# Delta net chunk inverse: from doubling levels on TensorE to a block series whose 32x32 diagonal blocks VectorE solves column by column

## The reference

```python
xn = rmsnorm(h, attn_norm)
proj = xn @ w_in               # columns: q, k, v, z, a, b, sB, sC, sh, gA, gB
qkv = silu(causal_dwconv(qkv, width 4)); q, k = l2norm(q), l2norm(k)
G = jnp.cumsum(g, axis=-1)     # log decay in a chunk
decay = jnp.exp(jnp.where(lower, G[..., :, None] - G[..., None, :], -jnp.inf))
A = jnp.where(strict, beta[..., :, None] * kk * decay, 0.0)
sol = lax.linalg.triangular_solve(eye + A, rhs, left_side=True, lower=True)
u, w = sol[..., :Dv], sol[..., Dv:]
...                            # per chunk: u_new, output o, state S; then o = rmsnorm(o) * silu(z)
h = h + mixed @ w_o            # then SwiGLU FFN and a per-layer embedding
```

## Time and profile before

| | |
|---|---|
| median of 3 runs | 2937.09 us (2936.52 to 2937.82) |
| profiled execution (its span) | 2936.8 us; the profile gives no other time for this execution |
| period of the loop `groups` | 150.7 us, 7 times |
| busy in the span | PE 97%, PE's weight loads 95%, DVE 59%, ACT 46%, POOL 5% |

### The profile page before, as it was taken

The page is one execution under the profiler, slowest core; times in us unless marked ns, Lnnn a source line. Parts: engine busy times, 40 slices in busy tenths (PEclk is TensorE's granted clock), DMA queues, the critical chain, the costliest instruction groups (busy, mean ns, idle before and its releaser), DMA issues.

```text
span 2936.8 us, 60061 instructions
## 1 busy us (share of the span) xinstructions
PE 2862.6 (97%) x22925; PEld 2803.5 (95%) x22925; DVE 1725.2 (59%) x3042; ACT 1342.0 (46%) x1999; POOL 141.7 (5%) x240
## 2 busy tenths in 40 slices
PE   6999999999999999999999999999999999999997
PEld 5999999999999999999999999999999999999997
DVE  5665565656566565655333555555677666776664
ACT  5434444444444443434334444334556544665563
POOL 2000000000000000000000000000011000100000
PEclk9999999999999999999899999999999999999998
DMA  6534343434333333437665555574799666995551
GB/s 208 169 98 126 107 127 110 125 105 121 111 117 118 111 112 119 123 117 217 182 197 171 175 172 172 172 261 145 223 315 294 209 207 188 317 300 183 174 169 63
DMA packets 435904, 494.13 MB, mean 168 GB/s; under 512 B 17329, under 2 KB 419498, under 8 KB 432866
## 3 DMA queue, kind: packets, MB, share of 16 engines
q1 hardware_dynamic: 415264, 415.42, 45.3%
q0 software_dynamic: 19872, 75.90, 8.2%
q10 hardware_dynamic: 578, 0.19, 0.0%
HBM read 467.67 MB, written 24.36 MB: 168 GB/s over the span
## 4 chain that ended last, share of the span: by engine, by line
PE 93%; DVE 3%; ACT 1%; issue 1%; DMA 0%; DVEq 0%; ACTq 0%
PE bank L579 93%; DVE wlo L1116 1%; ACT xhi L853 0%; DVE cacc L1272 0%; DVE GW L1255 0%; DMA vrow<-in_gdn_norm 0%; PE bank L627 0%; ACT whi L839 0%; DVE h L1534 0%; DVE xlo L1137 0%; ACT pp L993 0%; DVE hpro L1129 0%; DVE o_all L1260 0%; DVE cin L1333 0%; DVE xlo L1144 0%
## 5 line engine op out<-in xcount | busy, mean ns | idle before, releaser
L579 PE MATMUL bank<-xhi,whi 128*128 128x264 f32 x5520 | 1614.7, 293 | 43.2 <-issue 23.0
L579 PE MATMUL bank<-xlo,whi 128*128 128x264 f32 x5520 | 1584.1, 287 | 0.0
L579 PE MATMUL bank<-xhi,wlo 128*128 128x264 f32 x5520 | 1580.7, 286 | 0.0
L1116 DVE TENSOR_TENSOR wlo<-raw,whi 128x1024 fp32r<-128x1024 f32 x828 | 1007.8, 1224 | 799.2 <-ACT whi L839 797.2
L839 ACT ACTIVATE whi<-raw 128x1024 fp32r<-128x1024 f32 x828 | 874.4, 1059 | 788.7 <-PE bank L579 785.0
L579 PEld LDWEIGHTS bank<-xhi,whi 128*128 128x128 f32 x5520 | 1056.8, 191 | 61.0 <-issue 53.7
L579 PEld LDWEIGHTS bank<-xlo,whi 128*128 128x128 f32 x5520 | 1057.2, 192 | 4.5 <-issue 3.8
L579 PEld LDWEIGHTS bank<-xhi,wlo 128*128 128x128 f32 x5520 | 1054.8, 191 | 0.0
L579 PE MATMUL bank<-GW 128*128 128x128 f32 x2432 | 294.1, 275 | 0.0
L579 PEld LDWEIGHTS bank<-GW 128*128 128x128 f32 x2432 | 283.2, 192 | 0.0
L579 PE MATMUL bank<-ahi,wlo 128*128 128x264 f32 x704 | 200.1, 284 | 0.0
(11 more groups left out here) (259 smaller groups left out, 1655.6 us busy)
## 6 DMA issues: line engine op xcount, KB each, us to landing
raw<-in_w_in SPq DMA_DIRECT2D x356, 512.0 KB, 3.7
raw<-in_w_ffn_gate SPq DMA_DIRECT2D x88, 512.0 KB, 4.5
raw<-in_w_ffn_up SPq DMA_DIRECT2D x88, 512.0 KB, 4.8
raw<-in_w_ffn_down SPq DMA_DIRECT2D x96, 384.0 KB, 3.8
raw<-in_w_gdn_out SPq DMA_DIRECT2D x64, 512.0 KB, 3.5
chunkS<-in_state_gdn POOLq DMA_DIRECT2D x16, 1024.0 KB, 7.4
raw<-in_w_sconv_out SPq DMA_DIRECT2D x32, 512.0 KB, 3.6
raw<-in_w_o SPq DMA_DIRECT2D x32, 512.0 KB, 3.6
```

The source lines that it names most:

```text
L579: return pe.matmul(out, lhsT, rhs, start=start, stop=stop)
L1116: dve.tensor_tensor(wlo[:, at_ % SPLIT, :, :], raw[:, at_ % RAW, :, :], f32(whi[:, at_ % SPLIT, :, :]), ALU.subtract).then_inc(lo_ready, 1)
```

## The change

**Inverse.** The strictly lower triangular matrix of a chunk is split in its four 32x32 diagonal blocks and the rest. The diagonal blocks of all 8 systems (4 heads, 2 chunks) are laid over the 128 partitions by a DMA round trip through DRAM on ACT's queue (`blk_store`, `blk_load`). DVE solves them by forward elimination with 31 pivots, each as a multiplication and an addition over two halves of the columns (4 instructions for a pivot, 124 in all), four pivots after each of the pieces 17 to 24. POOL brings the result back through DRAM (`solution_out`) as `DT`, and PE multiplies it with what lies below the diagonal blocks (`pt`); the right hand side is then applied as a short series of four terms in that product (`pt0`, `pe0`, `pf0` for chunk 0, `pt1`, `pe1`, `pf1` for chunk 1).

**Order.** Pairs in the loop come as q, k, v0, v1, z, sC, sh, z. The tables have two parts: `cur` for the head group whose columns this iteration streams (pieces 9 to 31) and `prev` for the one before (pieces 0 to 6). **Tiles.** `GW` gives way to `E`, `Tt`, `QK`, `Nn`, `PT`, `DT`, `blk`, `sol`, `prod`; the weight ring shrinks from 8 to 4 slots.

```diff
-RAW = 8
+RAW = 4
...
+SB = 32
+QC = 8
...
-QKVS = ("v0", "v1", "q", "k")
+def layer_pairs(gx):
+    return [qkvpair(k, gx) for k in ("q", "k", "v0", "v1")] + [zpair(0, gx), spair("sc", SC0, gx), spair("sh", SH0, gx), zpair(1, gx)]
...
-LEVELS = {p: (p - 3,) for p in range(8, 20)}
-PE_STEP = {0: (0,), 1: ("decay",), 2: (1,), 5: (3,), 7: (4,), **LEVELS, 20: (17, 23), 21: (18,), 22: (19,), 23: (20,),
-           24: (21,), 26: (22,)}
...
+PE_STEP = {"cur": {9: ("decay",), 10: ("sums",), 12: ("kkqk",), 14: ("nturn",), 18: ("tails",), 19: ("vturn",), 26: ("pt",),
+                   27: ("pt0",), 28: ("pe0",), 29: ("pf0",), 30: ("s1",), 31: ("ks",)},
+           "prev": {0: ("t1",), 1: ("pt1",), 2: ("pe1",), 3: ("pf1",), 4: ("o1",), 5: ("osum",), 6: ("sct",)}}
+ACT_STEP = {"cur": {10: ("squares",), 11: ("root", "exps"), 13: ("kcopy",), 14: ("blk_store",), 15: ("ncopy",), 16: ("blk_load",),
+                    19: ("stage",), 20: ("vcopy",), 26: ("t0c",), 28: ("f0c",), 30: ("s1c",)},
+            "prev": {0: ("t1c",), 2: ("f1c",), 4: ("osq",), 5: ("oroot",), 7: ("sct",)}}
+DVE_STEP = {"cur": {9: ("gsel",), 10: ("exponents",), 12: ("qkn",), 13: ("lt",), 26: ("mask",), 27: ("e0",), 28: ("ktok",),
+                    29: ("u0",), 31: ("r",)},
+            "prev": {1: ("e1",), 3: ("u1",), 4: ("s2",), 7: ("o",)}}
+PER_PIECE = 4
+for n in range(-(-(SB - 1) // PER_PIECE)):
+    b = 17 + n
+    DVE_STEP["cur"][b] = DVE_STEP["cur"].get(b, ()) + (f"solve{n}",)
...
 # PE
+elif slot == "pt":
+    pe.wait_ge(tails_staged, gr + 1)
+    pe.wait_ge(g["vcopied"], gr + 1)
+    pe.wait_ge(g["dt_in"], gr * 64 + 64)
...
 # ACT
+elif slot == "blk_store":
+    act.wait_ge(g["lt"], gr + 1)
+    for b in range(4):
+        act.dma_start(blk_d[:, b, :, :].rearrange("m j i -> j m i"), ...).then_inc(g["blk_stored"], 16)
+elif slot == "blk_load":
+    act.wait_ge(g["blk_stored"], gr * 64 + 64)
+    for q in range(4):
+        act.dma_start(blk[SB * q:SB * q + SB, :, :]..., ...).then_inc(g["blk_in"], 16)
...
 # DVE
+elif slot.startswith("solve"):
+    if n0 == 0:
+        dve.wait_ge(g["blk_in"], gr * 64 + 64)
+        for hc in halves:
+            chain.inc(dve.tensor_copy(sol[:, hc, :], unit[:, hc, :]))
+    for j in range(n0, min(n0 + PER_PIECE, SB - 1)):
+        n = SB - 1 - j
+        for hc in halves:
+            chain.settle(dve, but=1)
+            chain.inc(dve.tensor_tensor(prod[:, hc, 0:n], blk[:, j, j + 1:SB]..., sol[:, hc, j:j + 1]..., ALU.mult))
+        for hc in halves:
+            chain.settle(dve, but=1)
+            m = chain.inc(dve.tensor_tensor(sol[:, hc, j + 1:SB], sol[:, hc, j + 1:SB], prod[:, hc, 0:n], ALU.add))
...
 # POOL
+def solution_out(grp):
+    pool.wait_ge(g["solved"], grp + 1)
+    for q in range(4):
+        pool.dma_start(sol_d[:, :, QC * q:QC * q + QC, :]..., sol[SB * q:SB * q + SB, :, :]...).then_inc(g["sol_stored"], 16)
+    pool.wait_ge(g["sol_stored"], grp * 64 + 64)
+    for b in range(4):
+        pool.dma_start(DT[SB * b:SB * b + SB, :, SB * b:SB * b + SB], ...).then_inc(g["dt_in"], 16)
```

More of the change, by code:

```diff
@@ L242, in trunk @@
         g = {n: sem("g_" + n) for n in (
-            "squares", "gsel", "sums", "log", "gb", "root", "dt", "qkn", "kkqk", "turned", "copied",
-            "lt", "lt_turned", "vturned", "x", "y", "ycopied", "xy", "u0", "u0s", "s1", "s1c", "ks", "r",
-            "expo", "xinit", "u1", "u1s", "o1", "s2", "stored", "osq", "osum", "olog", "oroot", "o")}
+            "squares", "gsel", "sums", "log", "gb", "root", "expo", "dt", "qkn", "kkqk", "kcopied", "lt", "nturned", "ncopied",
+            "blk_stored", "blk_in", "solved", "sol_stored", "dt_in", "vturned", "vcopied", "pt", "masked",
+            "t0", "t0c", "pt0", "e0", "pe0", "f0c", "pf0", "u0", "s1", "s1c", "ks", "r",
+            "t1", "t1c", "pt1", "e1", "pe1", "f1c", "pf1", "u1", "o1", "s2", "stored",
+            "osq", "osum", "olog", "oroot", "o")}
         gate_scaled = sem("gate_scaled")
@@ new lines, in gdn @@
+                    m.then_inc(g["t1"], 1)
+                elif slot == "pt1":
+                    pe.wait_ge(g["t1c"], gr + 1)
+                    apply(B[4], E, 1).then_inc(g["pt1"], 1)
+                elif slot == "pe1":
+                    pe.wait_ge(g["e1"], gr + 1)
+                    apply(B[5], Tt, 1).then_inc(g["pe1"], 1)
+                elif slot == "pf1":
+                    pe.wait_ge(g["f1c"], gr + 1)
+                    apply(B[4], E, 1).then_inc(g["pf1"], 1)
+                elif slot == "o1":
+                    pe.wait_ge(g["u1"], gr + 1)
+                    for i, s in enumerate(heads):
@@ L692, in extra @@
             def extra(ph, it, j):
-                gr = group_of(ph, it)
-                if gr is not None:
-                    for step in PE_STEP.get(j, ()):
-                        gdn(step, gr)
-                elif ph.name == "first" and j == 9:
+                for step, gr in steps(PE_STEP, ph, it, j):
+                    gdn(step, gr)
+                if ph.name == "first" and j == 9:
                     pe.wait_ge(rows_ready, 1)
@@ L788, in work @@
                     pe.wait_ge(x_in, 16 * (BLK + 1))
-                    for kt in range(DT):
+                    for kt in range(DTL):
                         if kt >= 8:
@@ L1001, in extra @@
             def extra(ph, it, j):
-                gr = group_of(ph, it)
-                if gr is not None:
-                    for step in ACT_STEP.get(j, ()):
-                        gdn(step, gr)
-                elif ph.name == "pgate_last" and j < 7:
+                for step, gr in steps(ACT_STEP, ph, it, j):
+                    gdn(step, gr)
+                if ph.name == "pgate_last" and j < 7:
                     if j == 0:
@@ L1132, in norm_split @@
                     copy(0)
-                for kt in range(DT):
-                    if psum and kt + 1 < DT:
+                for kt in range(DTL):
+                    if psum and kt + 1 < DTL:
                         copy(kt + 1)
@@ L1430, in extra @@
             def extra(ph, it, j):
-                gr = group_of(ph, it)
-                if gr is not None:
-                    for step in DVE_STEP.get(j, ()):
-                        gdn(step, gr)
-                elif ph.name == "first" and j == 9:
+                for step, gr in steps(DVE_STEP, ph, it, j):
+                    gdn(step, gr)
+                if ph.name == "first" and j == 9:
                     dve.wait_ge(tok_turned, 1)
@@ L1529, in work @@
                     norm_split(XR["ple"], 336)
-            walk(dve, work, (mine,), dve_per)
+            walk(dve, work, ((mine, dve_per), (chain, {ph.name: 2 + 4 * (SB - 1) if ph.name == "groups" else 0 for ph in phases})))
             norm_mean(3)
-            for kt in range(DT):
+            for kt in range(DTL):
                 dve.scalar_tensor_tensor(out=h[:, kt, :], in0=h[:, kt, :], scalar=vec[:, 352 + kt:353 + kt], in1=rstd[:, :],
```

596 lines of the change are left out of this document (304 added, 292 removed).

## The result

The changed kernel takes 3024.23 us (3020.13 to 3026.22, 4 runs) against 2937.45 us of the kernel before in the same job: ratio 1.0281, 95% interval 1.0263 to 1.0299. One execution of the kernel before, of 14549 us, counts as slow and is left out of the ratios of its job. The prediction was 3000 us, range 2955 to 3085. The profiled execution has a span of 3023.6 us against 2936.8.

What follows compares the result with a forecast made beforehand. TensorE, busy 97%, was taken as the bound. An iteration: -22.4 removed work + 5.1 + 12.7 + 7.5 waits + 6.0 clock = +8.9; seven make +62 on 2936.8, so 3000 us, range 2955 to 3085.

Steps and rivals of the forecast that it cites:

- Removed work: TensorE's inverse: 104 fp32 matmuls fewer at 0.215 us each, saving 22.4 us for a head group.
- Wait A: Ahead of kkqk: TensorE waits 5.1 us for the scaled q and k, behind VectorE's v0 evacuation.
- Wait B: Ahead of pt: TensorE waits 12.7 us for DT, after a 17.7 us solve and a 10.5 us DMA round trip.
- Wait C: Ahead of decay: TensorE waits 7.5 us for gsel, late in VectorE's queue.
- Clock: Behind each of the three waits the lowered TensorE clock loses 2.0 us, 6.0 us an iteration.
- The loop's period: Loop over head groups: each iteration grows by 8.9 us, to a period near 159.6 us; seven make +62.
- First and last group: `first` and `last_group` together do one head group, without the wait for gsel: -0.6 us.
- The ring: Weight ring of 4 slots: 15.6 us left for landing, so no cost taken; as rival +25 us, 3025, chance 0.1.
- rival 3: VectorE's solve pays for each of its waits, 27 us: +9.6 in each of 8 groups, 3077 us; chance 0.2.
- The rival of the other sign: Waits ahead of kkqk and decay: one or both absorbed, only pt's stays; -7.7 us a group, 2875 us; chance 0.08.

Runs made afterwards that it cites:

- all steps moved: Changed kernel with pt and steps behind it two pieces later, gsel at piece 7, solve from piece 16 with four pivots a piece: 2897.54 us, ratio 0.9862.
- the early scaling and the late z: All steps moved, plus q and k scaling one piece earlier and ScalarE's first z evacuation behind the next pair's second rounding: 2866.60 us, ratio 0.9756.
- the fastest kernel: The kernel with all steps moved, the early scaling and the late z, but five pivots a piece in place of four: 2853.97 us, ratio 0.9722.

## Why the prediction was right, and where it was off

- **Removed work.** 104 matmuls a group, 208 records: exactly seen. Their price comes out of one iteration before and one after (us, then TensorE's busy time, clock last but two):

```profile
467.00:617.80 150.80, 148.65 (x1195) 143.31 (x1193) 91.20 (x200) 64.08 (x98) 7.42 (x14) 0.99 0.38 116
```

```profile
572.38:732.77 160.39, 134.21 (x984) 127.26 (x984) 100.28 (x302) 61.51 (x88) 11.83 (x22) 0.89 0.39 114
```

  Slices of 1 us show 1.7 us of TensorE's work lost to the lower clock in the first and 10.8 in the second. At full speed the busy time would be 147.0 and 123.4, so I estimate the removed work at some 23.5 us where the forecast took 22.4.
- **Wait A**, 5.1: measured 4.9. **Wait B**, 12.7: 12.2, from a solve of 17.8 us (17.7 forecast) and a round trip of 9.5 (10.5 forecast; two landings of 3.7 were taken, and the second was 2.0). **Wait C**, 7.5: 7.4. Following each engine's queue from one event with durations from rows hit all three. Taking the cause of B away removed it; moving the steps of A and C removed them, but brought smaller waits one or two steps on.
- **Clock.** I took 2.0 a wait. It was 2.3 behind B; behind C, where two long fp32 products follow, the windows show 0.50 from 572.4 to 579 and 0.64 in the next, 3.7 us; behind A 0.50 in all six slices from 594 to 600 and 0.90 in the next, 3.1. That is 9.1 in this iteration against the 6.0 of the sum: this term was a third too small. The loss of 1.7 at the loop's end stayed, as forecast. The "2.1" for a longer idle stands in no row; behind the idle at 57 to 62 us of the kernel before the slices give 2.3.
- **The loop's period.** This iteration, 160.4, is 10.3 us over the mean of before, 150.1. The idle time of TensorE in it is 26.2 us (24.5 in the three waits), and with the clock's 10.8 that is 37.0 where the mean of before has 3.1 (150.1 less 147.0): 33.9 - 23.5 = 10.4. On the mean of six iterations the period grew by 9.7, against 8.9 forecast. That it came so near is partly luck: the clock was 3.1 dearer, and the removed work 1.1 and the waits 0.8 cheaper for the change than in the sum.
- **First and last group**, -0.6 forecast: 68.3 - 7 x 9.7 = 0.4.
- **The ring** is the term that was mis-sized: "I take nothing" for it. Outside the head groups the changed kernel lost 6.8 + 8.3 + 3.6 = 18.7 us, and the same cut cost 18.5 us in the kernel before; this is three quarters of the gap between 3000 and 3024. The rest is 0.8 us in each of 7 iterations and 1.0 in the first and last group. The step that failed was to compare 15.6 us of slack with the landings between 2010 and 2800 us only, at most 13.5. The phase of w_o has a longer one (22.0 in the trace of before). And the slack itself does not hold everywhere: at the start the landing was 10.3 us, shorter than 13.5, but the load could be issued only at 30.13 us, when the first piece had been rounded and subtracted, and TensorE had no seven pieces of work ahead of it. I had priced stalls in the FFN and the loop instead. In the phases with head groups the ring alone cost 1.0 us, next to nothing, as forecast.
- **Small slips in the prediction.** The lower end of its range takes 9 us for a cheaper clock, where 0.5 us at 23 waits is 11.5. For rival 3, 27 us for the solve are 9.3 over 17.7, not 9.6. The idle ahead of the clock loss of the earlier trace rows is 2.15 us in the timeline, not 2.4.
- **Rivals.** That the solve pays its whole record in each instruction did not happen. For the long ones its starts follow the rule from the earlier trace rows, 0.195 us for 124 elements where the rule gives 0.196. The shortest stay at 0.11 instead of falling to 0.07: the row of 28 elements (four blocks by seven) below starts 0.22 us ahead of the next, for two instructions, and so does the row of 4 elements.

```profile
640.88 0.28 DVE L1281 TENSOR_TENSOR prod<-blk,sol 128x28 f32<-128x28 f32 x2
641.10 0.29 DVE L1285 TENSOR_TENSOR sol<-sol,prod 128x28 f32<-128x28 f32 x2
```

Each of them lasts about 0.18 us, but 0.11 us is its price. By the Trainium skill, "VectorE: DVE Perf Modes", on the TRN2 errata, the estimate for one is (28 + 151)/0.96 = 186 ns: the record's length agrees, the distance of starts in two interleaved chains does not. The rival of the other sign (fewer waits, 2875) was not this kernel, but the experiments built it: with all waits shortened the same work takes 2854 us. The break-even that the prediction gave, 22.4 us of waits and clock in a group, was the right test.

For the moved kernels my forecasts were too low by 33 us (all steps moved) and 25 us (with the early scaling and the late z). There I had kept the landing of `DT` as it was in the changed kernel, and it took 5.2 to 5.3 us instead of 2.0. How much of the 33 and 25 us this accounts for was not measured.

## What to carry to other kernels

Work taken off the bounding engine is worth its time only if the results that replace it come back before the in-order queues want them: follow each queue from one event, and compare the sum of new waits and clock losses with the work saved. When a wait is found, try to move its consumer later as well as to make its producer faster; two pieces of delay gave 79 us here, a denser producer 4 (11 in the head groups). When a buffer ring is made smaller to pay for tiles, look for the longest landing in every phase of the program and at its start, where the slack is not yet built up, and not only where the change is.

## What the runs showed of the hardware

- The same small DMAs (128-byte pieces back from DRAM) landed in 2.0 to 2.2 us where the weight stream had paused or was ending, and in 4.0 to 5.3 us where it ran (medians). A round trip measured behind a stall is too cheap an estimate for the version without the stall.
- Waits of about 7, 5 and 12 us each brought the granted clock to 0.50. Behind the waits of 2.4 us for `DT` in the fastest kernel its first products had their full-speed length at the median, 275 ns (six of the eight groups), where they had 421 in the changed kernel:

```profile
L625 PE MATMUL bank<-DT,Nn x128: 275/275/464, 174.0 to 1132.5; 128*128 128x128 f32 x128
```

- The length of an idle stretch alone does not decide it. In the kernel before an idle of 2.15 us at a loop's end brought 0.52 and 0.50, and one of 2.94 us an iteration later, up to 733.66, left 1.00 in all slices. In the changed kernel one of 1.67 us, up to 683.75, was followed by 0.76, 0.50, 0.50 and 0.53. And in the last pass of the kernel before the clock fell at 1449 us behind 13 us in which TensorE was busy throughout (two windows, clock last but two). What decides it stays open.

```profile
1436.00:1449.00 13.00, 13.00 (x112) 13.00 (x111) 4.75 (x6) 6.19 (x7) 0.00 (x0) 1.00 0.67 198
1449.00:1453.00 4.00, 4.00 (x23) 4.00 (x22) 0.94 (x1) 0.24 (x1) 1.15 (x1) 0.57 0.43 113
```
